# Low parts of layer 0's output weights: stored once, then loaded

## Time and profile before

| | us |
|---|---|
| median of 3 runs | 1915.11 (1911.62 to 1917.10) |
| profiled execution | 1912.01 |
| its span, first to last instruction | 1910.3 |
| TensorE busy | 1789.3 (94%) |
| POOL busy | 614.0 (32%) |
| VectorE busy | 840.3 (44%) |
| POOL's subtraction L88, whole program | 315.9 in 129 instructions |
| layer 0's output product, three groups | 547.3 to 778.9 |

### The profile page before, as it was taken

How to read it: one execution, slowest core, us unless ns; L and a number is a source line. 1 busy time by engine, 2 the same in 40 slices (tenths; PEclk the granted TensorE clock), 3 DMA queues, 4 the chain that set the end, 5 groups by cost and what they waited for, 6 DMA issues and landing times. The chain is left out here.

```text
span 1910.3 us, 31602 instructions
## 1 busy us (share of the span) xinstructions
PE 1789.3 (94%) x12416; PEld 1460.6 (76%) x12416; DVE 840.3 (44%) x1215; ACT 509.5 (27%) x988; POOL 614.0 (32%) x514
## 2 busy tenths in 40 slices
PE   5999999999999999889999999789999999999698
PEld 2999999999987766689999999645666665665476
DVE  2720604407253768441101020266666666665443
ACT  3210101101121222220000010145555555455321
POOL 2422223233268878322223233211111111112340
PEclk8999999999999999899999999899999999999899
DMA  9223333231266444244333353388888998895651
GB/s 345 79 88 106 94 103 124 93 118 62 90 212 223 144 154 134 77 115 126 99 95 91 93 182 114 122 281 299 318 309 303 310 327 292 298 337 169 247 183 61
DMA packets 204814, 334.97 MB, mean 175 GB/s; under 512 B 37121, under 2 KB 138138, under 8 KB 202307
## 3 DMA queue, kind: packets, MB, share of 16 engines
q1 hardware_dynamic: 173475, 289.55, 45.7%
q10 hardware_dynamic: 31192, 43.40, 6.5%
HBM read 287.26 MB, written 45.63 MB: 174 GB/s over the span
## 5 line engine op out<-in xcount | busy, mean ns | idle before, releaser
L100 PE MATMUL ps<-actH,w_hi_a 128*128 128x352 f32 x1656 | 362.4, 327 | 0.0
L100 PE MATMUL ps<-actH,w_lo_a 128*128 128x352 f32 x1656 | 357.0, 323 | 0.0
L100 PE MATMUL ps<-actL,w_hi_a 128*128 128x352 f32 x1656 | 356.4, 323 | 0.0
L86 POOL CAST w_hi_a<-w_raw_a 128x1024 fp32r<-128x1024 f32 (+1 forms) x129 | 135.8, 1053 | 676.4 <-PE ps L100 554.8
L88 POOL TENSOR_TENSOR w_lo_a<-w_raw_a,w_hi_a 128x1024 fp32r<-128x1024 f32 (+1 forms) x129 | 315.9, 2449 | 10.3
L100 PEld LDWEIGHTS ps<-actH,w_hi_a 128*128 128x128 f32 x1656 | 280.1, 189 | 13.6 <-issue 13.4
L100 PEld LDWEIGHTS ps<-actH,w_lo_a 128*128 128x128 f32 x1656 | 284.3, 188 | 0.0
L100 PEld LDWEIGHTS ps<-actL,w_hi_a 128*128 128x128 f32 x1656 | 281.2, 188 | 0.0
L2064 DVE COPY KT<-ps 128x512 f32<-128x512 f32 x128 | 88.2, 690 | 211.0 <-PE ps L1827 210.0
L1827 PE MATMUL ps<-ident,K 128*128 128x128 f32 x1024 | 140.1, 281 | 23.6 <-DMA K<-in_cache_k_dram 6.6
L1749 POOL TENSOR_SCALAR diag<-ident,rinv 128x128 f32<-128x128 f32 x128 | 75.8, 605 | 266.7 <-DVE rinv L2012 266.7
(11 more groups left out here) (244 smaller groups left out, 2293.9 us busy)
## 6 DMA issues: line engine op xcount, KB each, us to landing
K<-in_cache_k_dram SPq DMA_DIRECT2D x128, 512.0 KB, 5.9
V<-in_cache_v_dram SPq DMA_DIRECT2D x128, 512.0 KB, 5.3
w_raw_a<-in_a_out_w_dram SPq DMA_DIRECT2D x48, 512.0 KB, 3.6
ada<-in_ada_w_dram SPq DMA_DIRECT2D x16, 1024.0 KB, 7.5
w_raw_a<-in_a_in_w_dram SPq DMA_DIRECT2D x32, 512.0 KB, 5.8
g_d<-g ACTq DMA_DIRECT2D x16, 528.0 KB, 2.7
mov_t<-g_d SPq DMA_DIRECT2D x16, 528.0 KB, 4.6
ada<-in_ada_w_dram SPq DMA_DIRECT2D x16, 512.0 KB, 4.6
```

The source lines that it names most:

```text
L86: pool.tensor_copy(high, raw).then_inc(w["hi_ready"], 1)
L100: mm = pe.matmul(acc[:, c, 0:CH], wt[:, j % SPL, k, :], act[:, k0 + k, c * CH:(c + 1) * CH], start=first and k == 0 and s == 0, stop=last ...
```

## The change

The low part of weight k is the same in all three groups. A new DRAM buffer `low_d` holds it. `kept(j)` says which jobs store theirs: even k in group 0, odd k in group 1. `loaded(j)` says which jobs load it in place of the subtraction: even k in group 1, every k in group 2. So all 16 are subtracted in group 0, the 8 odd ones again in group 1, and none in group 2. The casts (high parts) and the raw loads stay as they are, three times each.

Stores and loads are issued by SyncE. In iteration j it issues the raw load of j, then the store of j-2 if that is kept, then the load of j-2's low part if that is loaded, then what it issued before (mov, G, x_in). The load waits until job j-2-SPL has been used (its buffer is free) and until the store is down. The last two loads stand after the loop, ahead of the page table's. TensorE waits for the low part's load before the first matmul of a loaded job. POOL, before it subtracts into a buffer whose previous content is kept, waits for that store. For a loaded job the cast itself increments `split`, so the counter `hi_ready` runs behind by the number of loaded jobs (`fewer`).

```diff
+        def kept(j):
+            g, k = divmod(j - N_IN, nk)
+            return 0 <= j - N_IN < N0 - N_IN and (g == 0 and k % 2 == 0 or g == 1 and k % 2 == 1)
+
+        def loaded(j):
+            g, k = divmod(j - N_IN, nk)
+            return 0 <= j - N_IN < N0 - N_IN and (g == 1 and k % 2 == 0 or g == 2)
...
+        def keep_low(sp, j):
+
+            sp.wait_ge(w["split"], j + 1)
+            sp.dma_start(low_d[(j - N_IN) % nk], w["lo"][:, j % SPL].rearrange("p a n -> p (a n)").bitcast(F32)).then_inc(s_lowst, 16)
+
+        def load_low(sp, j):
+
+            k = (j - N_IN) % nk
+            sp.wait_ge(w["used"], j - SPL + 1)
+            sp.wait_ge(s_lowst, 16 * kept_up_to(max(x for x in range(N_IN, j) if kept(x) and ((x - N_IN) % nk == k or x == j - SPL))))
+            sp.dma_start(w["lo"][:, j % SPL].rearrange("p a n -> p (a n)").bitcast(F32), low_d[k]).then_inc(s_lowld[j % SPL], 16)
...
                         stream_weight(sp, w, j, jobs[j])
+                        if kept(j - RAW):
+                            keep_low(sp, j - RAW)
+                        if loaded(j - SPL):
+                            load_low(sp, j - SPL)
                         if g == 0 and k < nk - 4:
...
+                for j in range(N0 - SPL, N0):
+                    load_low(sp, j)
                 sp.dma_start(pt[:, :], page_table.rearrange("(a b) g -> a (b g)", a=1)).then_inc(s_pt, 16)
...
-                split_range(pool, w, jobs, N_IN, N0 + 2)
+                for j in range(N_IN, N0):
+                    pool.wait_ge(w["landed"][j % RAW], 16 * (j // RAW + 1))
+                    pool.wait_ge(w["used"], j - SPL + 1)
+                    raw, hi, lo = (w[n][:, j % r].rearrange("p a n -> p (a n)") for n, r in (("raw", RAW), ("hi", SPL), ("lo", SPL)))
+                    pool.tensor_copy(hi, raw).then_inc(w["split"] if loaded(j) else w["hi_ready"], 1)
+                    if not loaded(j):
+                        pool.wait_ge(w["hi_ready"], j + 1 - sum(loaded(x) for x in range(N_IN, j)))
+                        if kept(j - SPL):
+                            pool.wait_ge(s_lowst, 16 * kept_up_to(j - SPL))
+                        pool.tensor_tensor(lo, raw, hi.bitcast(F32), ALU.subtract).then_inc(w["split"], 1)
+                split_range(pool, w, jobs, N0, N0 + 2, sum(loaded(x) for x in range(N_IN, N0)))
...
                         pe.wait_ge(w["split"], j + 1)
+                        if loaded(j):
+                            pe.wait_ge(s_lowld[j % SPL], 16 * loads_up_to(j))
```

More of the change, by code:

```diff
@@ L75, in stream_weight, with split_range @@
         w["landed"][j % RAW], 16)
-def split_range(pool, w, jobs, lo, hi):
+def split_range(pool, w, jobs, lo, hi, fewer=0):
     for j in range(lo, hi):
@@ L86, in split_range @@
         pool.tensor_copy(high, raw).then_inc(w["hi_ready"], 1)
-        pool.wait_ge(w["hi_ready"], j + 1)
+        pool.wait_ge(w["hi_ready"], j + 1 - fewer)
         pool.tensor_tensor(low, raw, high.bitcast(F32), ALU.subtract).then_inc(w["split"], 1)
@@ L161, in build @@
     g_d = scratch("g_d", (KA, P, T))
+    low_d = scratch("low_d", (KA, P, D))
     x1_d = scratch("x1_d", (TT, P, D))
@@ L642, in stage_front @@
         s_in = [sem(f"s_in_{tag}{i}") for i in range(4)]
+        s_lowst, s_lowld = sem("s_lowst"), [sem(f"s_lowld{i}") for i in range(SPL)]
         s_lead = [sem(f"s_lead_{tag}{i}") for i in range(4)]
@@ L653, in stage_front, with kept_up_to, loads_up_to @@
         N0 = len(jobs)
+        def kept(j):
[4 more added lines that the diff above has]
+            return 0 <= j - N_IN < N0 - N_IN and (g == 1 and k % 2 == 0 or g == 2)
+        def kept_up_to(j):
+            return sum(kept(x) for x in range(N_IN, j + 1))
+        def loads_up_to(j):
+            return sum(loaded(x) for x in range(N_IN, j + 1) if x % SPL == j % SPL)
+        def keep_low(sp, j):
[6 more added lines that the diff above has]
+            sp.dma_start(w["lo"][:, j % SPL].rearrange("p a n -> p (a n)").bitcast(F32), low_d[k]).then_inc(s_lowld[j % SPL], 16)
         a = Arena(rows_at)
@@ L903, in _ @@
                 split_range(pool, w, jobs_in, 2, len(jobs_in))
-                split_range(pool, w, jobs, N_IN, N0 + 2)
+                for j in range(N_IN, N0):
[9 more added lines that the diff above has]
+                split_range(pool, w, jobs, N0, N0 + 2, sum(loaded(x) for x in range(N_IN, N0)))
                 normed.pool(pool, normed.last_parts(0, KD))
-                split_range(pool, w, jobs, N0 + 2, N0 + LAST_KV + 4)
+                split_range(pool, w, jobs, N0 + 2, N0 + LAST_KV + 4, sum(loaded(x) for x in range(N_IN, N0)))
                 pool.memset(one[:, :], 1.0).then_inc(s_cst, 1)
@@ L916, in _ @@
                                    pattern=[[NT, NB], [0, NH]], channel_multiplier=-1).then_inc(s_cst, 1)
-                split_range(pool, w, jobs, N0 + LAST_KV + 4, len(jobs))
+                split_range(pool, w, jobs, N0 + LAST_KV + 4, len(jobs), sum(loaded(x) for x in range(N_IN, N0)))
             @block.tensor
```

## The result

| | before | changed |
|---|---|---|
| median of 4 runs, us | 1916.11 (1911.62 to 1917.76) | 1968.45 (1964.52 to 1971.89) |
| profiled execution's span, us | 1910.3 | 1965.1 |
| output product, first matmul to K/V's first, us | 231.6 | 284.5 |

The ratio is 1.028 (1.026 to 1.030): 2.8% slower. Forecast were 1951 us, 1927 to 1976. The time lies in the range, but the loss is 52 us where the sum said 36. It lies between the forecast and the rival in which every gap brings the slow clock (1974), for whose sake the range reached that far.

What follows compares the result with a forecast made beforehand. TensorE was taken to bound the kernel, POOL close behind. Six terms along the output product (1.3 + 2.1 + 8.6 + 7.4 + 8.5 + 8.3) summed to 36.2 us more, giving 1951 us, range 1927 to 1976.

Steps and rivals of the forecast that it cites:

- the rival in which every gap brings the slow clock: Steady pairs of groups 1 and 2: each new TensorE gap costs 1.65 us, 14 pairs give 23 us, 1974; chance 0.17.
- What bounds and what is relieved: Output product: TensorE sets the pace, POOL close behind; 24 subtractions removed give back about 9 us of stretched jobs.
- The chain of the late load: Groups 1 and 2: cast, raw issue, low issue and landing in sequence make two jobs take 10.5 us.
- terms 4 and 6: Ends of groups 1 and 2: low parts' loads queue behind x_in and other transfers, +7.4 and +8.3 us.
- E: Time mark: end of a group's k = 12 work with its transposes, from which starts at the group's end are counted.
- Term 2: From job (0,14) into group 1: the late-load chain takes 10.4 us in place of 8.3, +2.1 us.
- S(1,0): Start of TensorE's work on weight 0 of group 1 (groups from 0), put at 10.4 us after weight 14 of group 0.
- Terms 3 and 5: Groups 1 and 2 up to k = 12: six pairs plus 1.5 us for stretched casts, 64.7 us each, +8.6 and +8.5.
- Term 1: Group 0: one more 512 KB store at k = 8 delays the next raw load, +1.3 us.
- Fast landing: Low parts land as fast as loads standing alone, 3.5 us for 4.45, pair 9.6; 1934 us, chance 0.15.
- Hidden loads: Loads hide behind the matmuls and POOL's relief counts, 9 us gained; 1906 us, chance 0.05.

Runs made afterwards that it cites:

- experiment 4: Changed kernel with the low part's load ahead of the raw load and waited for only after the 12 high-part matmuls; 1920.20 us, ratio 1.004.
- 7: Kernel before, with x_in loads spread, G and postg loads later in group 0, page-table wait only ahead of its use; 1904.38 us, ratio 0.995.
- 8: Changed kernel with low part's load ahead, high-part matmuls first, x_in spread, G and postg later, page-table wait later; 1902.40 us, ratio 0.994.
- 1: Changed kernel with the low part's load of j-2 issued ahead of the raw load of j, same transfers; 1938.87 us, ratio 1.014.
- 2: Changed kernel with the 12 high-part matmuls first and the low part's load waited for only then, same DMA order; 1932.31 us, ratio 1.009.
- experiment 6: Changed kernel with the three x_in loads at each group's end issued one by one, behind the low parts' loads; 1952.25 us, ratio 1.020.
- fifth: Changed kernel with 20 extra matmuls before the low-part wait of even k from 2 on, groups 1 and 2; 2006.72 us, ratio 1.048.
- ninth: Changed kernel with 16 extra matmuls before the low-part wait at k = 2 and 4 of groups 1 and 2 only; 1970.60 us, ratio 1.030.
- third: Changed kernel with the 16 stores kept but no loads, every low part subtracted again as before; 1919.88 us, ratio 1.004.

## Why the prediction was right or wrong

**What bounds and what is relieved: right.** TensorE set the pace, and the subtractions taken off POOL were worth a few us: 9 were forecast for their stretched jobs, 5.4 showed once little else stood in the way (experiment 4), 4.3 between experiments 7 and 8. So the size was about twice what the runs show.

**The chain of the late load: right, shown.** Its steps measured 6.10 us from the cast's start where 6.01 was forecast; TensorE's waits end with the low part's load; and issuing it earlier or needing it later takes back some 27 and 34 of 52 us (experiments 1 and 2).

**The ends of groups 1 and 2 (terms 4 and 6): right**, within 0.2 us each, and the cause, x_in ahead of the low part, shown by experiment 6. The steps between hold too: (1,15) was forecast at E + 19.3 and (2,0) at E + 25.6, and they came at 19.5 and 25.8.

**Term 2, into group 1: mis-sized.** The text took S(1,0) as S(0,14) + 10.4 from the steady chain. It was 14.0. The step that failed is the landing: the raw load of (1,0) was read 5.8 us after its issue, which put the cast 1.0 us late, and the low part landed after 7.0, not 4.45. Group 0 issues its x_in loads at k = 15, and the term left them out of the queue; but whether they are the cause is not shown. In the fifth and ninth kernels, with the same transfers, the stretch took 12.0 and 12.1 us, and with x_in spread 12.35. So some 1.6 of the 3.6 us come each time and 2 vary from one execution to the next, and what holds the loads up no run separates.

**Terms 3 and 5, the steady pairs: mis-sized by the clock.** The term took pairs at full clock (10.5 us). The rival "the clock falls in every pair" at 0.17 was true of about half: three jobs in each stretch at some 1.6 us are 5 us, of the 5.7 and 6.0 by which the terms were short. Landings above 4.45 added some 1.6 us in each stretch (4.3 to 5.3 each), and the 1.5 us for stretched casts was more than came (0.5 and 0.9). The text gave the steady stretch of before, at full clock, "1.2 us gaps"; its waits there are 0.7 to 0.9 us, so the new gaps lay further from it than it took them to be. That the lower clock took this time is read from the durations of the same matmuls; the two attempts to remove it alone (experiments 5 and 9) failed, and the second gave the time expected of latency alone, so its price is not shown by an experiment.

**Term 1, group 0: mis-sized.** 2.7 for 1.3. One more store at k = 8 lengthened the wait from 1.46 to 2.62 us, as argued, but (0,9) then had four slow pairs. That wait is 2.30 to 4.38 us in the eight kernels that issue the same transfers up to there, so the 1.2 us more of this execution lie at the low end.

**The other rivals.** "Fast landing" did not come: the median in group 2 was 4.5, as for mov. "Hidden loads" is what the eighth kernel is, and even there it gains nothing measurable over leaving the change out, since 7 has the same time.

**The range held partly by luck.** It was drawn to cover the slow clock in every pair; half of that came, and terms 1 and 2, short by 5.0 us together, fell into the same margin.

**What stays open.** Why a gap near 2 us sometimes lowers the clock and sometimes does not, and what delays the loads into (1,0).

## What to carry to other kernels

A transfer in place of computation pays only if it is issued early. Here, with two buffers of which one is in use, "when the buffer is free" plus a cast and a load that nobody needs yet came to 6.1 us, and the work it should hide behind is one job of 4.2 to 4.5. First order the queue by what is needed next, and use the operand that comes late last; then ask whether the computation that is saved was on the path at all. Here it hardly was: moving loads that the change does not touch (x_in, G, postg) gains as much alone as with it, as far as these runs can tell.

## What the runs showed of the hardware

- Gaps of TensorE and its clock. In the kernels without a fill, matmuls of the product went on at full clock after every wait of 1.90 us or less. After waits from 1.95 to 2.35 us some did and some did not: 2.02 us at (1,6) of the changed kernel had four slow pairs behind it, 2.24 us at (1,6) of the sixth and 2.35 us at (2,15) of the third had none. After 2.54 us and more the slow pairs were there each time: one pair starts 0.85 us after the other where 0.46 is usual, at a granted clock of 0.51 in 643.0 to 646.5 us of the changed kernel (the lower of the two levels, 1.2 for 2.4 GHz). Timeline of PE of the changed kernel at (1,6):

```profile
665.90 0.70 PE L1095 MATMUL ps<-w_hi_a,actH 128*128 128x512 f32 x2 [2.02 <-DMA w_lo_a<-low_d]
666.44 0.67 PE L1095 MATMUL ps<-w_lo_a,actH 128*128 128x512 f32 x2
666.91 1.05 PE L1095 MATMUL ps<-w_hi_a,actL 128*128 128x512 f32 x2
```

- POOL and VectorE slow each other. VectorE's instruction on y takes 3.40 us beside POOL's subtraction and 1.28 to 2.06 in the eighth kernel, the longer ones beside a cast. POOL's cast and subtraction take 1.04 and 2.41 us alone, 2.04 and 3.24 beside VectorE.
- A 512 KB load landed 3.5 us after its issue when it stood alone, 3.9 with the last load some 3 us ahead of it (median, group 2 of experiment 1), 4.5 right behind one load, 5.2 with a load and a store 1.6 and 1.3 us ahead (median, group 1 of experiment 1), and 10.2 behind six transfers.
